# Sample attention's keys, scores and softmax placed among the prompt attention's pairs of heads

## What is computed

```
mp, sp = mixer_prompt(rmsnorm(yp, norm_mix[l]), w_in[l], ...)      # prompt attention, banded and dilated
ms, ss = mixer_sample(rmsnorm(ys, norm_mix[l]), cache_a_k[l], cache_a_v[l], cache_b_k[l], cache_b_v[l], ...)
yp = yp + mp @ w_out[l]
ys = ys + ms @ w_out[l]

def gather_attention(q, k_all, v_all, idx, dist, table):           # sample attention
    ...
    logits = jnp.einsum('bthgd,btmhd->bhgtm', q, kg).astype(jnp.float32) * ATTN_SCALE + bias
    lse = jax.nn.logsumexp(logits, axis=-1)
    p = jnp.exp(logits - lse[..., None])
    o = jnp.einsum('bhgtm,btmhd->bthgd', p.astype(vg.dtype), vg)
```

## Time and profile before

| | us |
|---|---|
| median of 3 runs | 1201.89 |
| lowest and highest | 1200.39, 1202.03 |
| the profiled execution's own time | 1202.3 |
| its span, first to last instruction | 1200.5 |
| PE busy in the span | 1069.8 (89%) |
| DVE busy, ACT busy | 587.9 (49%), 469.8 (39%) |

### The profile page before, as it was taken

One profiled execution on the slowest core, in us unless ns is written; L12 is line 12 of the kernel. 1 busy time (PEld: TensorE's weight loads), 2 busy tenths in 40 slices (PEclk: granted clock), 3 DMA queues, 4 the chain that ended last, 5 costly groups with the idle time before them and its releaser, 6 DMA issues. The chain is left out here.

```text
span 1200.5 us, 16318 instructions
## 1 busy us (share of the span) xinstructions
PE 1069.8 (89%) x5923; PEld 868.2 (72%) x5924; DVE 587.9 (49%) x972; ACT 469.8 (39%) x736; POOL 145.3 (12%) x133
## 2 busy tenths in 40 slices
PE   5799999999899998878999549999999999999960
PEld 3699999998556666546888337877877777778750
DVE  5411113420166653325335565664599966649534
ACT  5311111101366652224123223554378645547324
POOL 0000000000100000000000011312234342223420
PEclk8699999999899998988999759999999999999995
DMA  6125111222440007866322554578699965789438
GB/s 221 64 54 203 49 53 53 71 65 78 122 131 1 2 1 239 249 186 205 131 106 97 200 221 120 193 265 280 226 380 397 377 209 200 273 291 395 118 70 314
DMA packets 104161, 207.34 MB, mean 173 GB/s; under 512 B 12648, under 2 KB 47249, under 8 KB 104075
## 3 DMA queue, kind: packets, MB, share of 16 engines
q1 hardware_dynamic: 96764, 179.89, 42.0%
q0 software_dynamic: 7344, 26.74, 9.2%
HBM read 175.75 MB, written 36.55 MB: 177 GB/s over the span
## 5 line engine op out<-in xcount | busy, mean ns | idle before, releaser
L545 PE MATMUL bank<-xT_hi,w_hi 128*128 128x384 f32 (+1 forms) x432 | 96.2, 331 | 5.4 <-DVE w_rest L408 5.4
L545 PE MATMUL bank<-xT_rest,w_hi 128*128 128x384 f32 (+1 forms) x432 | 95.7, 330 | 0.0
L545 PE MATMUL bank<-xT_hi,w_rest 128*128 128x384 f32 (+1 forms) x432 | 94.5, 327 | 0.0
L1864 POOL DMA_INDIRECT x_rows<-y_out,out_id x24 | 64.7, 2694 | 212.1 <-DVE rows L1919 195.3
L1748 DVE TENSOR_TENSOR down_rest<-w_down,down_hi 128x2048 fp32r<-128x2048 f32 x32 | 71.9, 2288 | 20.3 <-ACT down_hi L1743 19.4
L545 PEld LDWEIGHTS bank<-xT_hi,w_hi 128*128 128x128 f32 x432 | 74.1, 190 | 5.6 <-issue 5.6
L1972 PE MATMUL gate<-gate_hi,rowsT_hi 128*128 128x512 f32 x192 | 77.2, 402 | 0.7 <-ACT rowsT_hi L1878 0.7
L1973 PE MATMUL gate<-gate_rest,rowsT_hi 128*128 128x512 f32 x192 | 77.7, 405 | 0.0
L2006 PE MATMUL y<-down_hi,hidT_hi 128*128 128x512 f32 x192 | 76.8, 400 | 0.0
L1973 PE MATMUL up<-up_rest,rowsT_hi 128*128 128x512 f32 x192 | 75.6, 394 | 0.0
L1972 PE MATMUL up<-up_hi,rowsT_hi 128*128 128x512 f32 x192 | 75.2, 392 | 0.0
(11 more groups left out here) (278 smaller groups left out, 2087.2 us busy)
## 6 DMA issues: line engine op xcount, KB each, us to landing
w_gate<-in_w_gate SPq DMA_DIRECT2D x16, 2048.0 KB, 12.0
w_up<-in_w_up SPq DMA_DIRECT2D x16, 2048.0 KB, 11.9
w_down<-in_w_down SPq DMA_DIRECT2D x16, 2048.0 KB, 12.6
stage<-in_w_in SPq DMA_DIRECT2D x6, 1536.0 KB, 7.0
k_cache<-in_cache_b_k SPq DMA_DIRECT2D x8, 768.0 KB, 9.4
bias_scratch<-bias_one_row SPq DMA_DIRECT2D x1, 5800.0 KB
mixT<-in_x_prompt SPq DMA_DIRECT2D x8, 512.0 KB, 3.9
x<-in_x_prompt SPq DMA_DIRECT2D x8, 512.0 KB, 3.9
```

Source lines behind the costliest of these rows:

```text
L545: ins = nc.tensor.matmul(bank[3 * (n % 2) + i][:, 0:m], w_tiles(wt, n // CH)[:, k, cols], xt[:, k, c:c + m], start=(k == 0 and x == 0), st ...
L1864: nc.gpsimd.indirect_dma_start(out=io["x1"], out_offset=bass.IndirectOffsetOnAxis(ap=out_id[:, :], axis=0), in_=y_out[:, :], in_offset=Non ...
```

## The change

The B part's keys, scores and softmax no longer stand after the prompt but among its duos. The list `items` now holds the 40 duos and the 4 pairs: pair r stands behind duo 15, 22, 29 and 36. In each of the six duos before it, two key tiles are transposed (24 duos in all: 9 to 14, 16 to 21, 23 to 28 and 30 to 35), behind the duo's own transposes. They use the `turn` banks alone. ACT copies the even, DVE the odd key tile. The A part's key transposes stand behind duo 6. A pair's scores use `score[0]` and count as a long item. The exponentials of the four pairs stay in a new buffer `logit_s`; the division by the sum is moved to the copy of the values (ACT's `scale=`), so that the scaling on DVE goes. The matmul that spreads the sinks is replaced by a DMA. Behind the prompt there remain the A scores and, for each pair, the transposes of the probabilities, the values and the transposes of the result.

SP loads the keys 0 and 1 ahead of the small bias loads, all others during the prompt, each when its buffer's last user has been transposed. The values get more places: sequences 1 and 2 in the key buffers, 3 and 4 in `kT_s` (free when pair 3 is scored), 6 in `logit`, 5 in `V`, 7 in `v_cache` again. `w_out` is now loaded after the values of sequence 7, which wait for the values of pair 0.

```diff
+        A_KEYS, FIRST_KEYS, DUOS_PAIR = 6, 9, 7
+        def keys_beside(q):
+            r, x = divmod(q - FIRST_KEYS, DUOS_PAIR)
+            return [(2 * r + x // 3, 2 * (x % 3) + k) for k in range(2)] if 0 <= r < PAIRS and x < 6 else []
+        items = []
+        for q in range(DUOS):
+            items.append(("duo", q))
+            r, x = divmod(q - FIRST_KEYS, DUOS_PAIR)
+            if 0 <= r < PAIRS and x == 6:
+                items.append(("pair", r))
...
+            def score_banks(j):
+                free = j - 1 if long(j) or (j and long(j - 1)) else j - 2
+                if free >= 0:
+                    pe.wait_ge(biased, through[free])
...
+            def pair_scores(r):
+                score_banks(item_of["pair", r])
+                pe.wait_ge(q_blocked, HEADS)
+                wait_taken(pe, groups_of("ks", 2 * r + 1)[-1])
+                pe.wait_ge(new_k, 1 + 2 * r + 2)
...
-            scores(0)
-            for q in range(DUOS):
+            item_scores(0)
+            for j, (kind, q) in enumerate(items):
                 i, d = q // DUOS_TILE, q % DUOS_TILE
-                if q + 1 < DUOS:
-                    scores(q + 1)
+                if j + 1 < len(items):
+                    item_scores(j + 1)
+                if kind == "pair":
+                    continue
                 turn_probs(2 * q)
                 if q:
                     values(q - 1)
...
+                for b, k in keys_beside(q):
+                    turn_keys(b, k)
...
+            load_v(0)
+            for b in range(2, NB):
                 load_k(b)
-            for b in (0, 1):
+            for b in (1, 2):
+                sp.wait_ge(turned, groups_of("ks", NB - 3 + b)[-1] + 1)
                 load_v(b)
+            sp.wait_ge(scored, at_pair(PAIRS - 1))
+            load_v(3)
+            load_v(4)
...
+            load_v(6)
+            sp.wait_ge(valued, DUOS)
+            sp.dma_start(va_cache[:, :, :], io["cache_a_v"]).then_inc(va_loaded, 16)
+            load_v(5)
+            sp.wait_ge(valued, valued_of(0))
+            load_v(7)
```

More of the change, by code:

```diff
@@ L646, in attend @@
         k_loaded = [p.sem(f"k_loaded{i}") for i in range(2)]
-        v_loaded = [p.sem(f"v_loaded{i}") for i in range(2)]
-        last_v_loaded = [p.sem(f"last_v_loaded{i}") for i in range(2)]
+        v_loaded = [p.sem(f"v_loaded{i}") for i in range(PAIRS)]
         blanks = p.sem("blanks")
@@ L679, in unit, with at_unit, at_pair, long @@
             return i, 0, i + 1, False, s
-        def long(q):
-            return unit(2 * q)[2] > 4
+        A_KEYS, FIRST_KEYS, DUOS_PAIR = 6, 9, 7
[8 more added lines that the diff above has]
+                items.append(("pair", r))
+        through = []
+        for kind, _ in items:
+            through.append((through[-1] if through else 0) + (2 if kind == "duo" else 1))
+        SOFTMAXES = through[-1]
+        item_of = {item: j for j, item in enumerate(items)}
+        def at_unit(u):
+            return through[item_of["duo", u // 2]] - 1 + u % 2
+        def at_pair(r):
+            return through[item_of["pair", r]]
+        def long(j):
+            kind, x = items[j]
+            return kind == "pair" or unit(2 * x)[2] > 4
         def score_at(u):
-            q, x = u // 2, u % 2
-            return score[x] if long(q) else score[x][:, 512 * (q % 2):512 * (q % 2) + 512]
+            j, x = item_of["duo", u // 2], u % 2
+            return score[x] if long(j) else score[x][:, 512 * (j % 2):512 * (j % 2) + 512]
         def value_at(q):
@@ L737, in attend @@
             acts_upto.append(acts_upto[-1] + by_act(n))
-        def bank_key(n):
-            if groups[n][0] == "ks" and n // 2 % 2:
-                return "score", (groups[n][1] // 2 + 1) % 2, n % 2
-            return "turn", 0, n % 2
         def bank_of(n):
-            kind, s, half = bank_key(n)
-            return score[s][:, 512 * half:512 * half + 512] if kind == "score" else turn[half][:, :]
-        last_user, previous = {}, []
-        for n in range(len(groups)):
-            previous.append(last_user.get(bank_key(n), -1))
-            last_user[bank_key(n)] = n
+            return turn[n % 2]
         def wait_taken(eng, upto):
@@ L1171, in spread_recips, with item_scores @@
                 ins.then_inc(turned, 1)
-            scores(0)
-            for q in range(DUOS):
+            def item_scores(j):
+                kind, x = items[j]
+                if kind == "duo":
+                    scores(x)
+                else:
+                    pair_scores(x)
+            item_scores(0)
+            for j, (kind, q) in enumerate(items):
                 i, d = q // DUOS_TILE, q % DUOS_TILE
-                if q + 1 < DUOS:
-                    scores(q + 1)
+                if j + 1 < len(items):
+                    item_scores(j + 1)
+                if kind == "pair":
+                    continue
                 turn_probs(2 * q)
```

436 lines of the change are left out of this document (218 added, 218 removed).

## The result

| | before | after |
|---|---|---|
| time, us, median (lowest to highest) | 1201.96 (1200.39 to 1203.64) | 1218.95 (1214.75 to 1219.92) |
| ratio to before, 95% interval | 1 | 1.0139 (1.0114 to 1.0165) |
| span of the profiled execution, us | 1200.5 | 1213.0 |
| start of `attend` (first prompt scores) | 316.76 | 314.19 |
| prompt: from there to the last transposes of reciprocals | 137.4 | 198.0 |

The sign was right and the size was not: 1208.0 was forecast, 1216 was the upper end. The difference is in `attend`: 248.6 us instead of 233.2 in the profiled executions. That is 15.4 more, where the forecast had 6.1. Ahead of `attend` after was 2.6 us shorter, and the experts differ by 0.6. The profiled execution of after is the shortest of its four.

A forecast was written before the change was run, and what follows sets the result against it. PE was taken to bound the prompt, with idle time and half clock to gain in the sample part. Prompt 52.2 us longer, sample part 51.1 shorter, 5 of clock loss: 6.1 slower, 1208.0 us, range 1196.5 to 1216.

The forecast's parts named there:

- Moved work: In the prompt: key transposes 15.7, pair scores 16.2 and A-part key transposes 2.2 add 34.1 us of PE work.
- lost cover: In the prompt at the four pairs: a pair uses up work that covered the next duo's softmax; 6.2 us.
- New waits for the turn banks: In the prompt's 24 key duos: key transposes wait for DVE's copy to free their bank; 10.7 us, bounds 0 and 23.
- Credit of 2.1: In the prompt: keys ahead of scores fill waits already there; a third of 6.25 us idle, 2.1 us off.
- The pair's wait for the last copies: In the prompt at the four pairs: scores wait for the copies of the last keys; 3.3 us for the four.
- The clock in the prompt: In the prompt: the forecast's sum had nothing for a fall of the clock there.
- Rival 3: The clock falls in the prompt at gaps of up to 2.5 us; four pairs make 6.8 us, 1214.8 us; chance 0.13.
- What remains: Behind the prompt, to the sample part's last transposes: sample part shrinks by 51.1 us, 5 us of clock loss added back.
- Loads: Keys and `w_out` land before their use; both costed at nothing.
- The forecast's sign for a prompt of over 57 us more: If the prompt grows by over 57 us, rival 3 or 4 holds.
- under 46: If the prompt grows by under 46 us, the forecast's bank waits are wrong.
- rival 4: Loads come late: keys 0 and 1 queue behind bias loads, or `w_out` ends last; 1218 us; chance 0.05.

The follow-up runs named there:

- n3: The changed kernel with the sample key tiles still transposed on PE but never copied out; 1212.83 us, ratio 1.0098 to the kernel before.
- e12: The changed kernel with the pair items one duo later (behind duos 16, 23, 30 and 37) and nothing else; 1211.86 us, ratio 1.0087 to before.
- c0: The changed kernel once more, unaltered, for a second profile; median 1215.87 us, ratio 1.0120 to the kernel before.
- n2: The changed kernel without the four pair items in the prompt, key transposes kept; 1189.78 us, ratio 0.9922 to the kernel before.
- e1: The changed kernel with each duo's two key transposes set apart: even behind the previous duo's values, odd behind the next duo's scores; 1235.00 us, ratio 1.0288 to before.
- e5: The changed kernel with only the even key tile moved, behind the even unit's probability transposes and ahead of the previous duo's values; 1220.28 us, ratio 1.0182 to before.
- e10: The changed kernel with pairs one duo later, next duo's scores earlier at pairs, key tiles carried to the next duo and copied by ACT alone; 1204.86 us.
- e11: e9 and e10 together; 1201.74 us, ratio 1.0021 to the kernel before.
- n4: The changed kernel with neither key tiles nor pair items; 1159.54 us, ratio 0.9653 to the kernel before.
- e9: The changed kernel with pairs one duo later, next duo's scores earlier at pairs, and, behind the prompt, next pair's probability transposes ahead of this pair's values; 1202.37 us.

## Why the prediction was wrong, by its own steps

- **Moved work, 34.1.** Right: 1.8 for the A keys where 2.2 stood, and 22.4 for the pairs without keys, lost cover included, where 22.4 stood. (Six transposes of 0.65 at 24 places are 15.6, not 15.7.)
- **New waits for the turn banks, 10.7. This is the step that failed:** 16.4, or 16.7 from start to start. The kind of wait, its place and its releaser were right. The sizes were not, for two reasons. The first is what a stall costs beside its row. The forecast gave PE a pace of 0.33 for a key group throughout and stopped the count where "the second key group then waits 0.48"; at duo 9 that wait came out at 0.44, but what follows the group came 0.12 late as well, and so at every one of the 24 places. In the six long duos without reciprocals the first group came 0.74 to 0.87 late, where 0.7 stood. The second is one size for each kind of duo: 0.41 for the eight short ones without reciprocals, where the starts give 0.44 to 0.58 in four, 0.70 in two, and 0.96 and 1.49 at duos 24 and 34, at which DVE works off biases of long units before it copies. That the idle time of the rows (10.8) equals the forecast's 10.7 is chance, since the forecast had counted from start to start. The bounds beside the term, 0 and 23, held it, and the range made no use of the upper one.
- **Credit of 2.1.** Right: 2.3, or 2.6 from start to start.
- **The pair's wait for the last copies, 3.3, and lost cover, 6.2.** Right: 3.2 on top of keys and pairs, and 3.6 and 3.9 by n3 and e12. Of the cover, after's timeline has 0.94, 1.61 and 2.46 at pairs 0, 1 and 3, where 0.8, 1.5 and 2.5 stood, and at pair 2 the wait grew by 2.30 - 0.97 = 1.33, where 1.4 stood.
- **The clock in the prompt, 0. This failed too:** 3.4 us in after and in c0. Rival 3 had the price of one fall (1.7) and put four of them at the gaps of up to 2.5 at the pairs. There were two, and one of them had no such gap ahead of it. It was weighed as an alternative, not as a part of the sum, although the trace of before has no gap over 1.23 us in the prompt, and so nothing that speaks against a fall at 2.3. The Trainium skill, page "TensorE: Matmul & The Clock Gate", section "A second HAM failure mode: psum-queue depth-cycling", tells of another kernel, whose clock falls again and again with brief and frequent idling between groups. By that rule the 21 short stalls at the banks should have brought it down, and the trace doesn't agree: n2 has them all, at 1.00 from 340 to 480. In e1, where PE waited for key copies up to 2.1 us and far more often, it did fall, for 10.2 us in all.
- **What remains, 43.9 with 5 for the clock behind the prompt.** Right in the first profile (44.7), with 6.8 for the clock instead of 5 and 1 less for the work; about 2 longer in the second, by the clock.
- **Loads, nothing.** Right: no key transpose and no values waited for a load.

So of the missing 8.4 us 5.7 are the bank waits and 3.4 the clock, and all else together is 0.7 the other way. The forecast's sign for a prompt of over 57 us more named rivals 3 and 4 and pointed past the larger part: for the bank waits it had foreseen only that they be too small (under 46). Rival 3 itself didn't come, with 3.4 of its 6.8, and rival 4 not at all.

## What to carry to other kernels

Where a step is put among the work of an engine that is the bound, its price is its length plus a stall for each buffer that it has to wait for. Take the stall from start to start and not from the idle time of the row: here 0.5 us became 0.8. Whether a buffer comes free in time is set by the copying engine's queue: look at what stands ahead of the copy there, not at how much work lies between the two uses. Where an edit makes long waits on a busy TensorE, the half clock that may follow belongs into the sum as a term with its own bounds: in the prompts here it was 0 to 10.2 us. And a kernel that leaves work out can carry a cost of its own, like the 1.1 us of n2 and n4: look through its trace before taking differences.

## What the runs showed that was not expected

- 24 tile pairs placed further apart on TensorE cost 20.5 us more than placed together (e1), because of the order on DVE and ACT.
- 21 waits of 0.3 to 1.3 us left the granted clock at 1.00 from 340 to 480 (n2). With waits of up to 2.5 us at the pairs it fell in most kernels, in steps of 1.7 us, up to 10.2 us (e1), but not in e5, e10 and e11. Two executions of the same kernel had their two falls at different pairs.
- Behind the prompt the clock took 8.3 to 12.5 us, and two executions of one kernel lay 4 us apart (after and c0). A gain of that size can't be read there from one execution of each kernel (e9).
- A fill of 128x3104 on GpSimd and a copy of DVE beside it: the copy took 2.61 us, and 0.36 without (n2 and n4).
- The same program's executions differ by up to 8.6 us (1211.62 to 1220.22), by the length of the projections and the clock behind the prompt.
